# Both norms of the tail beside its projections, and the first columns of the down projection read back during the up projection

## What is computed

```python
def rmsnorm(x, w):
    xf = x.astype(jnp.float32)
    y = xf * lax.rsqrt(jnp.mean(xf * xf, axis=-1, keepdims=True) + EPS)
    return (y * w.astype(jnp.float32)).astype(x.dtype)

    ...
    y_ssm = y_ssm.reshape(bsz, L, D_INNER).astype(x.dtype) @ w_ssm_out
    ...
    merged = jax.nn.sigmoid(mg_ssm) * y_ssm + jax.nn.sigmoid(mg_gdn) * y_gdn
    x = x + merged @ w_o
    ...
def conv_ffn(x, s_conv, norm_w, w_up, conv_w, conv_b, w_down):
    h = rmsnorm(x, norm_w)
    gt, up = split_cols(h @ w_up, (D_FF, D_FF))
    gt, new_conv = causal_dwconv(gt, s_conv, conv_w)
    return x + (jax.nn.silu(gt + conv_b) * up) @ w_down, new_conv
    ...
    y = rmsnorm(x, norm_f_w)
```

## Time and profile before

| | |
|---|---|
| median of 3 runs | 3430.29 us |
| the profiled execution's own time | 3431.91 us |
| its span in the profile | 3429.7 us |
| mean granted clock of PE | 0.932 |
| PE busy | 3034.4 us, 88% of the span |
| DVE busy | 1549.1 us, 45% |
| ACT busy | 943.2 us, 28% |
| POOL busy | 375.4 us, 11% |
| HBM traffic | 244.00 MB read, 93.22 MB written |

### The profile page before, as it was taken

One profiled execution on the slowest core, in us unless ns is written; L12 is line 12 of the kernel. 1 busy time (PEld: TensorE's weight loads), 2 busy tenths in 40 slices (PEclk: granted clock), 3 DMA queues, 4 the chain that ended last, 5 costly groups with the idle time before them and its releaser, 6 DMA issues. The chain is left out here.

```text
span 3429.7 us, 52527 instructions
## 1 busy us (share of the span) xinstructions
PE 3034.4 (88%) x19132; PEld 2847.3 (83%) x19132; DVE 1549.1 (45%) x2356; ACT 943.2 (28%) x1868; POOL 375.4 (11%) x525
## 2 busy tenths in 40 slices
PE   3899999999999788888886786999869999997997
PEld 2899999999999677767775346999859999997996
DVE  5455555511111377778776535545242333323444
ACT  2232222311121244434443101333121111112332
POOL 1000000000000122322222323000000000000000
PEclk7899999999999899999998676999979999998998
DMA  2222222222242222234222515554302122115432
GB/s 76 80 88 100 88 88 94 94 100 88 88 134 100 73 61 62 62 78 104 62 61 54 181 74 205 183 193 155 115 2 82 56 75 73 57 62 213 173 127 93
DMA packets 223761, 338.94 MB, mean 99 GB/s; under 512 B 146296, under 2 KB 159336, under 8 KB 223248
## 3 DMA queue, kind: packets, MB, share of 16 engines
q1 hardware_dynamic: 217344, 312.00, 28.8%
q0 software_dynamic: 6288, 25.25, 2.0%
HBM read 244.00 MB, written 93.22 MB: 98 GB/s over the span
## 5 line engine op out<-in xcount | busy, mean ns | idle before, releaser
L534 PE MATMUL pps<-h_hi,pwh 128*128 128x358 f32 (+1 forms) x2112 | 688.4, 326 | 15.4 <-DVE pwl L599 15.4
L534 PE MATMUL pps<-h_lo,pwh 128*128 128x358 f32 (+1 forms) x2112 | 689.8, 327 | 0.0
L534 PE MATMUL pps<-h_hi,pwl 128*128 128x358 f32 (+1 forms) x2112 | 687.2, 325 | 0.0
L534 PEld LDWEIGHTS pps<-h_hi,pwh 128*128 128x128 f32 x2112 | 397.3, 188 | 15.8 <-issue 15.8
L534 PEld LDWEIGHTS pps<-h_hi,pwl 128*128 128x128 f32 x2112 | 398.8, 189 | 0.0
L534 PEld LDWEIGHTS pps<-h_lo,pwh 128*128 128x128 f32 x2112 | 397.6, 188 | 0.0
L1681 PE MATMUL u_ps<-f_hi,up_wh 128*128 128x358 f32 (+1 forms) x1056 | 344.5, 326 | 18.3 <-DVE up_wl L1673 18.3
L1681 PE MATMUL u_ps<-f_lo,up_wh 128*128 128x358 f32 (+1 forms) x1056 | 345.2, 327 | 0.0
L1681 PE MATMUL u_ps<-f_hi,up_wl 128*128 128x358 f32 (+1 forms) x1056 | 343.9, 326 | 0.0
L599 DVE TENSOR_TENSOR pwl<-pw,pwh 128x1024 fp32r<-128x1024 f32 x88 | 107.8, 1226 | 508.1 <-ACT pwh L547 501.5
L1681 PE MATMUL merge_ps<-merge_yh,merge_wh 128*128 128x358 f32 (+1 forms) x576 | 190.4, 331 | 30.6 <-DVE merge_yl L1830 22.7
(11 more groups left out here) (427 smaller groups left out, 5224.6 us busy)
## 6 DMA issues: line engine op xcount, KB each, us to landing
projected<-pO SPq DMA_DIRECT2D x88, 536.0 KB, 2.9
pw<-in_w_in SPq DMA_DIRECT2D x88, 512.0 KB, 3.7
merge_w<-in_w_out SPq DMA_DIRECT2D x72, 512.0 KB, 3.6
down_w<-in_w_down SPq DMA_DIRECT2D x48, 704.0 KB, 4.1
up_w<-in_w_up SPq DMA_DIRECT2D x44, 512.0 KB, 4.0
chunk<-projected SPq DMA_DIRECT2D x5, 3744.0 KB, 16.7
scan_chunk<-projected SPq DMA_DIRECT2D x5, 3744.0 KB
ffn<-uf SPq DMA_DIRECT2D x22, 536.0 KB, 3.0
```

Source lines behind the costliest of these rows:

```text
L534: ins = pe.matmul(ps[:, 3 * u + n, 0:cn], l[u][:, k, :], r[:, k, c0:c0 + cn], start=(k == 0 and a == 0), stop=(k == KD - 1 and a == 2))
```

## The change

**Residual.** The stage now goes by column group on the outside and by tile inside, 24 units (n, m) of 24 matmuls. The weights `w_o` are therefore loaded and split three times instead of once, one unit per 24 matmuls instead of per 72. `x` comes in three DMAs. After each unit DVE adds one tile of one group to `x`, ACT squares it, and POOL adds the square into `wo_acc`. When a group is done, the norm of that group (`norm(n)`: PE sums over the partitions, ACT makes `f_rstd`, DVE scales, ACT rounds, DVE subtracts) stands in every stream ahead of the last two tiles of the next group. Of the last group only `f_rstd` is made here; its scaling and splitting stand at the start of the **up** stage, and PE waits for them (`n_lo`) ahead of its third column group. The stage ffnnorm is gone.

**Up.** After round 11, and again after round 20, SP reads the tiles of the first column group that are already in DRAM back to `down_raw` (11 and 10 tiles); the last tile is read by POOL at the start of the down stage.

**Down.** `down_phase` takes the place of `deep_phase` here. Its start converts a half of the activation first and splits a weight unit behind it. After each tile ACT squares, POOL accumulates; `norm(n)` stands ahead of the last two tiles of the next group, and that of the last group at the end. DVE scales `x` in place, and SP stores a group in two halves. The stage lastnorm is gone. ACT loads the table set of Ln and Exp at the start of the residual and of the down stage.

The diff, cut to its core:

```diff
+def down_phase(nc, d, source, x, ones, raw):
...
+        def steps(eng, start, body, norm):
+
+            for n in range(3):
+                start(n)
+                with eng.Fori(0, pairs - 1) as i:
+                    for u in range(2):
+                        body(n, 2 * i + u, u, pairs * n + i, (KD * n + 2 * i + u) * nu)
+                if n:
+                    norm(n - 1)
+                for u in range(2):
+                    body(n, KD - 2 + u, u, pairs * (n + 1) - 1, (KD * (n + 1) - 2 + u) * nu)
+            norm(last)
...
+            def norm(n):
+                c0, cn = NCOL[n]
+                for half in range(2):
+                    ks = slice(KD // 2 * half, KD // 2 * (half + 1))
+                    sp.wait_ge(scaled.sem, scaled.at(n, KD // 2 * (half + 1)))
+                    sp.dma_start(d["y"][:, ks, c0:c0 + cn], x[:, ks, c0:c0 + cn]).then_inc(stored.sems[0], 16)
...
+            pool.dma_start(raw[:, 1, ku - 1, :], source[FT - 1, :, 0:CN]).then_inc(raw_in.sems[1], 16)
+            steps(pool, start, body, lambda n: None)
...
+            act.preload_act_table_set("natural_log_exp_and_others")
+            def convert(n, unit):
+
+                cn, k = NCOL[n][1], unit * ku
+                if unit or n:
+                    act.wait_ge(raw_in.sems[unit], raw_in.at(n if unit else n - 1))
...
+            def start(n):
+                for unit in range(nu if n == 0 else 0):
+                    convert(n, unit)
+                    ring.split_hi(act, unit, unit, unit, 1)
...
+                act.wait_ge(read[u].sem, read[u].at(rnd))
+                act.wait_ge(added[u].sem, added[u].ahead(rnd))
+                act.activation(sq[:, u:u + 1, 0:cn], x[:, bass.ds(m, 1), c0:c0 + cn], ACT.Square).then_inc(squared[u].sem, 1)
...
+            def norm(n):
+                c0, cn = NCOL[n]
+                dve.wait_ge(w_in.sems[0], w_in.at(0))
+                dve.wait_ge(rstd_done.sem, rstd_done.at(n))
+                for k in range(KD):
+                    dve.scalar_tensor_tensor(out=x[:, k, c0:c0 + cn], in0=x[:, k, c0:c0 + cn], scalar=w[:, k:k + 1],
+                                             in1=rstd[:, n % 2, 0:cn], op0=ALU.mult, op1=ALU.mult).then_inc(scaled.sem, 1)
...
-def residual_phase(nc, d, hi, lo, x):
+def residual_phase(nc, d, hi, lo, x, ones, f_hi, f_lo, w, rstd):
...
+            for n, (c0, cn) in enumerate(NCOL):
+                sp.dma_start(x[:, :, c0:c0 + cn], d["x"][:, :, c0:c0 + cn]).then_inc(x_in.sems[n], 16)
...
+            def body(n, m, u, rnd):
+                c0, cn = NCOL[n]
+                pe.wait_ge(read[u].sem, read[u].ahead(rnd))
+                pe.wait_ge(ring.lo_done.sem, ring.lo_done.at(KD * n + m))
+                ring.product(pe, u, ps[:, u, 0:cn], lambda k: hi[:, k, c0:c0 + cn],
+                             lambda k: lo[:, k, c0:c0 + cn]).then_inc(ring.used.sem, 1)
...
+            def body(n, m, u, rnd):
+                s = KD * n + m
+                if not (isinstance(s, int) and s + 1 >= 3 * KD):
+                    ring.split_hi(act, s + 1, 1 - u)
+                act.wait_ge(read[u].sem, read[u].at(rnd))
+                act.wait_ge(added[u].sem, added[u].ahead(rnd))
+                c0, cn = NCOL[n]
+                act.activation(sq[:, u:u + 1, 0:cn], x[:, bass.ds(m, 1), c0:c0 + cn], ACT.Square).then_inc(squared[u].sem, 1)
...
+            def norm(n):
+                root(n)
+                c0, cn = NCOL[n]
+                for k in range(KD):
+                    act.wait_ge(scaled.sem, scaled.at(n, k + 1))
+                    act.activation(f_hi[:, k, c0:c0 + cn], v[:, k % 4, 0:cn], ACT.Copy).then_inc(f_hi_done.sem, 1)
...
+                for k in range(3):
+                    scale(k)
+                for k in range(KD):
+                    if k + 3 < KD:
+                        scale(k + 3)
+                    dve.wait_ge(f_hi_done.sem, f_hi_done.at(n, k + 1))
+                    dve.tensor_tensor(f_lo[:, k, c0:c0 + cn], v[:, k % 4, 0:cn], f_hi[:, k, c0:c0 + cn].bitcast(F32),
+                                      ALU.subtract).then_inc(f_lo_done.sem, 1)
...
-def up_phase(nc, d, hi, lo, ffn):
+def up_phase(nc, d, hi, lo, ffn, x, w, rstd, first):
...
-            rounds(sp, body)
+            half, cn = FT // 2, NCOL[0][1]
+            with sp.Fori(0, half + 1) as j:
+                body(j)
+            sp.wait_ge(stored.sems[0], stored.at(half - 1))
+            sp.dma_start(first[:, 0, :, :], ffn[0:half, :, 0:cn].rearrange("k p n -> p k n")).then_inc(first_in.sems[0], 16)
+            with sp.Fori(half + 1, FT - 1) as j:
+                body(j)
+            sp.wait_ge(stored.sems[0], stored.at(FT - 2))
+            sp.dma_start(first[:, 1, 0:half - 1, :], ffn[half:FT - 1, :, 0:cn].rearrange("k p n -> p k n")).then_inc(
+                first_in.sems[0], 16)
+            body(FT - 1)
...
+                        if n == 2:
+                            pe.wait_ge(n_lo.sem, n_lo.at(0))
...
+            for k in range(KD // 2):
+                scale(k)
             ring.split_lo(dve, 0, 0)
+            for k in range(KD // 2, KD):
+                scale(k)
+            for k in range(KD):
+                dve.wait_ge(n_hi.sem, n_hi.at(0, k + 1))
+                dve.tensor_tensor(lo[:, k, c0:c0 + cn], v[:, k, 0:cn], hi[:, k, c0:c0 + cn].bitcast(F32), ALU.subtract).then_inc(n_lo.sem, 1)
...
-            norm_phase(nc, "ffnnorm", x, d["norm_ffn"], ones, hi, lo)
-            up_phase(nc, d, hi, lo, ffn)
-        deep_phase(nc, "down", ffn, FT // 2, 2, d["w_down"], (0, 0), x=x)
-        norm_phase(nc, "lastnorm", x, d["norm_f"], ones, out=d["y"])
```

316 lines of the change are left out of this document (249 added, 67 removed).

## The result

The changed kernel takes **3394.66 us**, the median of 6 runs (3389.8 to 3397.57), beside 3430.55 us for the kernel before, 6 runs on the same chip (3426.65 to 3438.32): a ratio of 0.989 (95% interval 0.988 to 0.991), 35.9 us less. The profiled execution took 3393.49 us, its span is 3391.7 us.

The account below looks back on a forecast made before the run. PE bounds the stages but idles between them, where the change aims. Gains 9.6 + 8.4 - 1.3 + 20.8 = 37.5 us give 3394.4 from the profiled execution, 3392.8 against the median, rounded to 3393 us; range 3381 to 3407.

Parts of the forecast that it names:

- Residual, steady state: Residual stage: chain of 3.6 to 3.7 us under PE's 3.92 per unit, no stall; 4.9 us of waits removed.
- late chain: Rival: residual chain exceeds PE's unit, costing 6.5 to 8 us over 11 pairs, 3399 to 3401 us; chance 0.2.
- Residual, start: Start of the residual stage: unit 2's weight load queues behind x; stall 5.3 us plus 2.1 cold clock, 7.4 us.
- Inner norms: Two norms inside the residual stage: each stalls PE 8.0 us, plus 2.1 cold and 0.65 sum; 21.5 us for both.
- lower bound of 6.4: Smallest stall in us forecast for one norm inside the residual stage, with the 7.3 us of the old instructions.
- Gap ahead of up: Last residual product to first of up: 11.1 us instead of 44.7, gain 33.6; net of residual losses 9.6 us.
- Read-back: During up: SP's reads put nothing on PE's path; weight loads behind them 0 to 4 us late for ACT.
- the cover: In up: PE needs the weight unit loaded behind the read-back 10 us after ACT's start; without this, once some 4 us.
- Start of down: Ahead of down: first product 11.0 us after SP's first issue instead of 19.4; gain 8.4 us.
- Norms inside down: Down stage: DVE's scaling fits while PE has two units ahead; only two sums, 1.3 us, are lost.
- End: Last product to end of span: 12.9 us instead of 33.7, with 4.3 for the last store; gain 20.8 us.
- slower case: Rival: residual weights, loaded three times, come late, costing 56 us over 11 pairs, kernel 3449 us; chance 0.03.

Follow-up runs that it names:

- the ACT run: The changed kernel with one more square of about 1.1 us, its result thrown away, ahead of each ACT square of the residual stage: 3404.76 us, one run.
- the two other runs with this stage unchanged: The changed kernel without the read-back during up, 3408.51 us, and the changed kernel with another start of the down stage, 3388.51 us.

## Why the prediction was right

The forecast was 3393 us; the 3394.66 lie within its range of 3381 to 3407. By its own steps:

1. *Residual, steady state: right.* No wait outside the four. In the rows above PE's last product ends at T = 2456.9 and the weights are ready at 2460.48, a chain of 3.6 us; over the stage's steady units it is 3.3 to 3.7. What the step got wrong is what a miss would cost: not the excess once per pair of units but the excess in every unit, as the ACT run shows. The rival "late chain" was priced at 6.5 to 8 us and would have been some 10. The room that saved the forecast is 0.1 to 0.5 us.
2. *Residual, start: right.* 5.05 us of stall against 5.3, and the load of unit 2 behind `x` is the reason: moving two pieces of `x` left 1.05 us of the wait. Two sizes in it were off and nearly cancel. The last piece of `x` landed 11.7 us after the stage's first product where the sum had 10.4, and the weights 1.3 us behind it where the sum had 2.4, a term for which no row stands. The clock behind the wait cost 5.45 - 3.93 = 1.5 us where 2.1 was charged.
3. *Inner norms: mechanism right, size 0.7 us too large each.* The sixteen instructions took 8.1 us instead of 8.9, and the root came at T + 2.3. The stalls are 7.30 and 7.28 instead of 8.0. The lower bound of 6.4 wasn't reached. Moving them away brought 16.9 us. The clock cost 5.68 - 3.93 = 1.8 us behind each, again less than 2.1.
4. *Gap ahead of up: right*, 11.0 against 11.1. With steps 2 and 3 the net is 12.6 us instead of 9.6: 1.7 of the 3.0 are the shorter stalls (19.6 instead of 5.3 + 16.0), and some 1.3 what the clock gave back sooner. This second part is luck of the profiled execution. In the two other runs with this stage unchanged the clock behind the three waits cost 7.2 to 7.4 us, not the 5.1 here or the 6.3 of the forecast, and the net is 9.7 us. With them the stage is as long as the forecast had it (126.1), because the stalls are 1 us smaller and the clock costs 1 us more.
5. *Read-back: right.* It costs nothing in up (520.6 against 520.3, and no wait of PE in it), and the cover held: ACT takes the first weights issued behind the read 10.0 us after their issue, without waiting, as in the earlier trace rows. They had landed after 9.1 us instead of 3.6, so 0.9 us was left. SP's and ACT's timelines:

```profile
2853.31 0.40 SPq L2270 DMA_DIRECT2D down_raw<-ffn  x1
2854.04 1.36 SPq L1656 DMA_DIRECT2D up_w<-in_w_up  x2
...
2864.03 1.09 ACT L1666 ACTIVATE up_wh<-up_w 128x1024 fp32r<-128x1024 f32 x1
```

6. *Start of down: right*, 11.1 us after SP's first issue against 11.0. That it is the read-back that makes it, the run without it shows; it is worth 13.5 us beside the rest of the change, more than the 8.4 of the sum, since the rest alone was 5.3 us slower than before.
7. *Norms inside down: right*, 1.3 us. PE waits for none of them.
8. *End: right*, 12.7 against 12.9. The store landed in 3.5 us and not 4.3. The estimate by the Trainium skill, "DMA: Bandwidth & Descriptors" (Anatomy of one DMA), was 3.6 us (3.7 with a KB of 1024 bytes) and is the nearer one here, although the page gives its fit for DMAs that GpSimd issues and this one is SP's. Up to the end of the scaling it is the 8.2 us of the forecast (3379.0 to 3387.2); what is left, 12.7 - 8.2 - 3.5 = 1.0, was reckoned at 0.4.

The sum was 37.5 us. The same stretches give 40.3 in the profiles, the 2.3 us ahead of the stage go off, and 38.0 are left. What nearly cancels is the smaller loss in steps 2 and 3 (+3.0) and the part ahead (-2.3), which is not the change's; that the total comes within 2 us is luck. The slower case had no part in it: the residual weights land in 3.5 us, as before.

## What to carry to other kernels

Work that is moved beside a busy engine is hidden only if it is cut to the room between the steps of its engine's stream. As one block of 8.1 us it stopped PE for 7.3 us, in pieces of 1 to 2 us for hardly anything; that was 17 us here, more than the 11.8 that the residual part had gained. When a chain is checked against its period, read in the streams what stands behind its last step. Double buffers give no slack where the add that starts the next chain waits in line behind the late step. A small load issued behind a large transfer is as late as the large one, in the same queue (12.4 us instead of 3.5) and from another one (7.1 us): order the issues by when their data are needed. And when a stage is rewritten, look for waits of the old one that are gone. The one that kept two weight loads off the activation's read is; with the read-back that costs PE nothing, and without it the read landed 3.6 us later.
